# Two of nine tiles get their experts from one pass over the whole table, and the other seven are summed in quarters of the TensorE array

## What is computed

```python
def peer_block(xb, w_q, pk_keys, u_tab, v_tab):
    q = (xb @ w_q).reshape(t, PEER_HEADS, 2, PEER_DHALF)
    s = jnp.einsum('thpd,hpkd->thpk', q, pk_keys).astype(jnp.float32)
    v1, i1 = lax.top_k(s[:, :, 0], PEER_TOPK)
    v2, i2 = lax.top_k(s[:, :, 1], PEER_TOPK)
    cand = (v1[..., :, None] + v2[..., None, :]).reshape(t, PEER_HEADS, PEER_TOPK * PEER_TOPK)
    best, flat = lax.top_k(cand, PEER_TOPK)
    ...
    idx = e1 * PEER_NKEYS + e2
    g = jax.nn.softmax(best, axis=-1)
    a = jax.nn.gelu(jnp.einsum('thkd,td->thk', u_tab[idx], xb))
    return jnp.einsum('thk,thkd->td', (g * a).astype(xb.dtype), v_tab[idx])
```

## Time and profile before

| stretch of the profiled execution, us | what it is | length, us |
|---|---|---|
| 0 to 1052 | `project`, `attend`, front of group 0 | 1052 |
| 1052 to 1851 | slots of tiles 0, 1 (128 ticks), front of group 1 (3 tiles) | 799 |
| 1851 to 2910 | slots of tiles 2 to 4 (192 ticks), front of group 2 (4 tiles) | 1059 |
| 2910 to 4203 | slots of tiles 5 to 8 (256 ticks) | 1293 |
| 4203 to 4212.5 | last sums and the last store | 9.5 |

### The profile page before, as it was taken

The page is one execution under the profiler, slowest core; times in us unless marked ns, Lnnn a source line. Parts: engine busy times, 40 slices in busy tenths (PEclk is TensorE's granted clock), DMA queues, the critical chain, the costliest instruction groups (busy, mean ns, idle before and its releaser), DMA issues.

```text
span 4212.5 us, 35633 instructions
## 1 busy us (share of the span) xinstructions
PE 3563.6 (85%) x11097; PEld 1824.6 (43%) x11097; DVE 2570.1 (61%) x5586; ACT 1487.6 (35%) x3959; POOL 1673.5 (40%) x1407
## 2 busy tenths in 40 slices
PE   8999999899889988768988878986777777787777
PEld 4545665588545454323333344442333332333222
DVE  2131456612868866958777875786775776776444
ACT  2111457611334435343443335443232233223222
POOL 0000000000337667576766667666333333333332
PEclk9999889999999999879999989998989999999999
DMA  4302320044999999899999999999999999999998
GB/s 139 113 20 71 117 71 21 21 155 151 418 418 415 419 412 420 320 421 421 421 420 420 414 416 414 421 405 418 421 421 421 417 416 415 417 413 418 421 422 348
DMA packets 238014, 1394.51 MB, mean 331 GB/s; under 512 B 25840, under 2 KB 53744, under 8 KB 84976
## 3 DMA queue, kind: packets, MB, share of 16 engines
q0 software_dynamic: 165888, 1208.03, 69.5%
q1 hardware_dynamic: 71936, 184.21, 12.0%
HBM read 1364.36 MB, written 28.70 MB: 331 GB/s over the span
## 4 chain that ended last, share of the span: by engine, by line
DMA 24%; PE 17%; POOL 16%; DVE 11%; issue 9%; ACT 2%; POOLq 0%; SPq 0%; DVEq 0%; ACTq 0%
DMA ring<-in_experts_dram,idx 24%; PE ps L1443 9%; POOL side L1333 9%; POOL ring L1322 7%; DVE ring L1717 4%; PE ps L1414 3%; PE ps L1366 2%; PE ps L1391 1%; PE ps L1376 1%; ACT diag L1540 1%; DVE hot L1598 1%; DVE cand L1583 1%; DVE hot L1594 1%; DVE idx L1602 1%; ACT wgt L1531 1%
## 5 line engine op out<-in xcount | busy, mean ns | idle before, releaser
L1443 PE MATMUL ps<-ring,diag 128*128 128x512 f32 x3648 | 1816.9, 643 | 568.9 <-ACT diag L1540 555.8
L1322 POOL DMA_INDIRECT ring<-in_experts_dram,idx x1152 | 1100.7, 955 | 2043.1 <-PE ps L1443 1285.4
L1717 DVE CUSTOM_DVE_ANT_0 ring<-ring,ps 128x1024 f32<-128x1024 f32 x1152 | 1382.8, 1219 | 766.8 <-DMA ring<-in_experts_dram,idx 751.1
L1443 PEld LDWEIGHTS ps<-ring,diag 128*128 128x128 f32 x3648 | 714.5, 203 | 1582.9 <-ACT diag L1540 809.3
L1524 ACT ACTIVATE act_<-hid 128x2 f32<-128x2 f32 x576 | 117.1, 203 | 1803.4 <-DVE hid L1717 1801.8
L1333 POOL TENSOR_TENSOR side<-side,ring 128x1024 f32<-128x1024 f32 x240 | 566.9, 2362 | 55.5 <-ACT ring L1545 50.8
L1366 PE MATMUL ps<-shared 128*128 128x256 f32 (+2 forms) x1152 | 401.0, 495 | 4.5 <-PEq L536 4.5
L1540 ACT ACTIVATE diag<-const,wgt 128x128 f32<-128x128 f32 x912 | 329.8, 396 | 19.4 <-PE ps L1443 0.5
L1366 PEld LDWEIGHTS ps<-shared 128*128 128x128 f32 x1152 | 225.1, 196 | 172.6 <-issue 117.4
L316 PE MATMUL ps<-shared,hT 128*128 128x512 f32 (+1 forms) x720 | 285.4, 552 | 1.8 <-DVE mhT L430 1.3
L1531 ACT ACTIVATE wgt<-act_,gw 128x1 f32<-128x1 f32 x1152 | 276.7, 287 | 20.6 <-ACT act_ L1524 0.4
(11 more groups left out here) (181 smaller groups left out, 2854.8 us busy)
## 6 DMA issues: line engine op xcount, KB each, us to landing
shared<-in_w_gate_o_dram SPq DMA_DIRECT2D x72, 768.0 KB
shared<-in_w_q_dram SPq DMA_DIRECT2D x24, 1024.0 KB
ring<-in_experts_dram,idx POOLq DMA_INDIRECT x1152
shared<-in_w_out_dram SPq DMA_DIRECT2D x12, 1024.0 KB
shared<-in_w_in_dram SPq DMA_DIRECT2D x5, 2048.0 KB, 8.1
o_x<-o_scratch SPq DMA_DIRECT2D x9, 768.0 KB
hT_scratch<-hT SPq DMA_DIRECT2D x9, 512.0 KB, 6.6
shared<-hT_scratch SPq DMA_DIRECT2D x9, 512.0 KB
```

The costliest lines, as they stand in the source:

```text
L1322: i = nc.gpsimd.indirect_dma_start(out=ring[:, j % RING, :], out_offset=None, in_=A["experts"], in_offset=bass.IndirectOffsetOnAxis(ap=idx ...
L1443: last = nc.tensor.matmul(acc[:, h, :], diag[:, (by_pe(j) - 1) % 4, :], ring[:, j % RING, DM + h * HB:DM + (h + 1) * HB], start=(j % SLOTS ...
L1717: last = nc.vector.tensor_tensor_reduce(out=u, in0=u, in1=xp, scale=1.0, scalar=0.0, op0=ALU.mult, op1=ALU.add, accum_out=hid[:, j % SLOTS ...
```

## The change

The groups are cut differently (0-1, 2-5, 6-8). Seven tiles (`SEQ`) are still gathered, slot by slot, so that there are 448 ticks in place of 576. Tiles 3 and 5 (`DENSE`) are not gathered. Their picks and gates are ranked as before, but each pick's gate is written to a table in DRAM, `gates_scratch`, 16384 experts by 2x128 tokens: POOL issues for each of the 2x128 slots an indirect transfer of 128 elements of 4 bytes with add (`scatter`). The table is cleared early by one transfer that ACT issues in `project`. Then, from tick `DENSE_AT` = 282 on, a third list of steps (`dense`) goes over all experts in 128 blocks of 128: SP loads `u` (from a host-made transposed copy, 512 KB a block), `v` (512 KB) and the gates (128 KB); PE multiplies `u` with both tiles' tokens (8 products of 256 columns), ACT applies gelu, DVE multiplies by the gates, and PE multiplies with `v` (4 products of 512 columns) into four PSUM banks.

The gathered tiles' sums change too. The side adds are gone: all slots go to PE. `diag` is now 128x64 (a folded diagonal: two 64x64 diagonals, one above the other), and a slot is four products of 64 rows by 64 columns by 512, one in each quarter of the array, in place of two of 128 by 128 by 512. The residual comes in through PE (`residual`), `finish` is a copy, and the stores put the quarters in order. The token's row is read from SBUF (`xp`), no longer from PSUM. The ring has 9 buffers. The ranking of tiles 3, 4 and 5 is packed into 28 ticks each.

```diff
-RING = 10
+RING = 9
 BATCH = 2
 NB = SLOTS // BATCH
-GROUPS = ((0, 1), (2, 3, 4), (5, 6, 7, 8))
-PARTS = (2, 3, 4)
-SIDES = (4, 4, 3, 3, 3, 0, 0, 0, 0)
-PLAIN = SLOTS // 2
-SIDE_AT = {0: (), 3: (1, 3, 6), 4: (1, 3, 5, 7)}
+GROUPS = ((0, 1), (2, 3, 4, 5), (6, 7, 8))
+PARTS = (2, 4, 3)
+SEQ = (0, 1, 2, 4, 6, 7, 8)
+DENSE = (3, 5)
+ALL = len(SEQ) * SLOTS
...
             act.wait_ge(pad_zero, 2)
+            nc.scalar.dma_start(S["G_d"].rearrange("(p r) t -> p (r t)", p=P).rearrange("p (a b) -> p a b", b=P),
+                                S["vsw"][:, 0, :].unsqueeze(1).to_broadcast([P, NK * NK * len(DENSE) // P, P])).then_inc(S["G_zero"], 16)
...
+DENSE_AT = 282
...
+    for i in range(2 * NB, DENSE_AT):
+        to = min(total[2], mid + -(-(total[2] - mid) * (i + 1 - 2 * NB) // (G2_TICKS - 4)))
+        out.append(to - done)
+        done = to
+    ticks = len(SEQ) * NB - DENSE_AT
+    for i in range(ticks):
+        to = total[2] + -(-DENSE_STEPS.steps * (i + 1) // ticks)
...
+RANK_AT = {1: (30, 48), 3: (2 * NB + 2, 28), 4: (2 * NB + 34, 28), 5: (2 * NB + 66, 28), 7: (4 * NB + 8, 36), 8: (5 * NB + 6, 48)}
...
+SPREAD_AT = ((2 * NB + 19, 8), (2 * NB + 83, 8))
+SPREAD = {}
+for _a, (_at, _gap) in enumerate(SPREAD_AT):
+    for _k in range(SLOTS):
+        SPREAD.setdefault(_at + _k // TOPK * _gap + _k % TOPK // 3, []).append((_a, _k))
...
+                def load_gates(b):
+                    if b >= 3:
+                        sp.wait_ge(d_gated, b - 2)
+                    sp.dma_start(dg[:, b % 3], G_d[b * P:(b + 1) * P, :]).then_inc(dg_in[b % 3], 16)
+
+                def load_values(v):
+                    if v >= 3:
+                        sp.wait_ge(d_summed, v - 2)
+                    src = x1_d[DENSE[v]] if v < ND else A["experts"][(v - ND) * P:(v - ND + 1) * P, DM:2 * DM]
+                    sp.dma_start(dv[:, v % 3], src).then_inc(dv_in[v % 3], 16)
...
+            def scatter(a, j):
+                if a == 0 and j == 0:
+                    pool.wait_ge(S["G_zero"], 16)
+                if j % (SLOTS // 2) == 0:
+                    pool.wait_ge(prepared[1], prepared_by(DENSE[a], j // (SLOTS // 2) + 1))
+                if j and j % TOPK == 0:
+                    pool.wait_ge(spread[a], 16 * j)
+                i = nc.gpsimd.indirect_dma_start(out=G_d.rearrange("e (t o) -> (e t) o", o=1),
+                                                 out_offset=bass.IndirectOffsetOnAxis(ap=spot[:, a, j:j + 1], axis=0),
+                                                 in_=gd[:, a, j:j + 1], in_offset=None, compute_op=ALU.add)
+                i.then_inc(spread[a], 16)
...
-            def accumulate(m, q):
-                pe.wait_ge(diags, m * NB + q + 1)
-                if q == 0 and m:
-                    pe.wait_ge(y_ready, m)
-                for j in range(m * SLOTS + q * BATCH, m * SLOTS + (q + 1) * BATCH):
-                    if sided(j):
-                        continue
+            def dense():
+                pe.wait_ge(h_in, 16 * (NT + ND))
+                pe.wait_ge(s_kept, PH * len(GROUPS))
+                for a in range(ND):
+                    pe.wait_ge(dv_in[a], 16)
                     for h in range(2):
-                        last = nc.tensor.matmul(acc[:, h, :], diag[:, (by_pe(j) - 1) % 4, :], ring[:, j % RING, DM + h * HB:DM + (h + 1) * HB],
-                                                start=(j % SLOTS == 0), stop=(by_pe(j) == by_pe(m * SLOTS + SLOTS - 1)), skip_group_check=True)
+                        last = nc.tensor.matmul(ps[:, 4 + 2 * a + h, :], ident, dv[:, a, h * HB:(h + 1) * HB], start=True, stop=False, skip_group_check=True)
+                    last.then_inc(d_summed, 1)
+                for t in range(D.steps):
+                    if t in D.scores:
+                        b = D.scores[t]
+                        pe.wait_ge(du_in[b % 3], 16 * (b // 3 + 1))
+                        if b >= 2:
+                            pe.wait_ge(d_gelued, b - 1)
+                        for k in range(KC):
+                            last = nc.tensor.matmul(ps[:, 2 + b % 2, 0:ND * P].rearrange("p (a t) -> p a t", t=P), du[:, b % 3, k, :],
+                                                    hx[:, 0:ND, k, :], start=(k == 0), stop=(k == KC - 1))
+                        last.then_inc(d_scored, 1)
+                    if t in D.values:
+                        b = D.values[t]
+                        v = b + ND
+                        pe.wait_ge(d_gated, b + 1)
+                        pe.wait_ge(dv_in[v % 3], 16 * (v // 3 + 1))
+                        for a in range(ND):
+                            for h in range(2):
+                                last = nc.tensor.matmul(ps[:, 4 + 2 * a + h, :], dw[:, b % 3, a * P:(a + 1) * P], dv[:, v % 3, h * HB:(h + 1) * HB],
+                                                        start=False, stop=(b == NK - 1), skip_group_check=True)
+                        last.then_inc(d_summed, 1)
+                    yield
+
+            advance = walk(front, dense)
...
+            def residual(n):
+                m = SEQ[n]
+                f = FRONTS[GROUP_OF[m]]
+                if n:
+                    pe.wait_ge(y_ready, n)
+                if f.final:
...
+                    x1 = side[:, n % 2]
+                for r in range(2):
+                    rows = slice(r * HD, (r + 1) * HD)
+                    for c in range(2):
+                        nc.tensor.matmul(acc[c * HD:(c + 1) * HD, r, :], ident[rows, r * HD:(r + 1) * HD], x1[rows, c * HB:(c + 1) * HB],
+                                         start=True, stop=False, skip_group_check=True)
+
+            def accumulate(n, q):
+                pe.wait_ge(diags, n * NB + q + 1)
+                if q == 0:
+                    residual(n)
+                for j in range(n * SLOTS + q * BATCH, n * SLOTS + (q + 1) * BATCH):
+                    for r in range(2):
+                        rows = slice(r * HD, (r + 1) * HD)
+                        for c in range(2):
+                            last = nc.tensor.matmul(acc[c * HD:(c + 1) * HD, r, :], diag[rows, j % 4, :], ring[rows, j % RING, DM + c * HB:DM + (c + 1) * HB],
+                                                    start=False, stop=(j % SLOTS == SLOTS - 1), skip_group_check=True)
                     last.then_inc(pe_done, 1)
...
+                    for j in range(n * SLOTS + q * BATCH, n * SLOTS + (q + 1) * BATCH):
+                        if j >= 4:
+                            act.wait_ge(pe_done, j - 3)
+                        last = nc.scalar.activation(diag[:, j % 4, :], folded, ACT.Copy, scale=wgt[:, j % SLOTS:j % SLOTS + 1])
                     last.then_inc(diags, 1)
...
+            def dense():
+                for t in range(D.steps):
+                    if t in D.gate:
+                        b = D.gate[t]
+                        dve.wait_ge(d_gelued, b + 1)
+                        dve.wait_ge(dg_in[b % 3], 16 * (b // 3 + 1))
+                        nc.vector.tensor_tensor(dw[:, b % 3], dw[:, b % 3], dg[:, b % 3], ALU.mult).then_inc(d_gated, 1)
+                    yield
+
+            def finish(n):
+                dve.wait_ge(pe_done, (n + 1) * SLOTS)
+                if n >= 2:
+                    dve.wait_ge(y_out[n % 2], 32 * (n // 2))
+                nc.vector.tensor_copy(side[:, n % 2], acc.rearrange("p a n -> p (a n)")).then_inc(y_ready, 1)
```

More of the change, by code:

```diff
@@ L1032, in paces @@
     out = [done]
[L1033 to L1044 removed]
+    start, mid = done, total[0]
```

458 lines of the change are left out of this document (255 added, 203 removed).

## The result

Four runs of the changed kernel gave 4236.21 to 4243.42 us, median 4239.75; the kernel before has 4214.81 beside them. The ratio is 1.0083 with a 95% interval of 1.0064 to 1.0101: 0.8% slower, where 2.6% faster was forecast. The run of 14265.89 us stands outside the comparison.

A forecast was written before the change was run, and what follows sets the result against it. Transfers were to bound ticks 0 to 127, transfers and DVE with scatters on top 128 to 281, PE the rest: 1052 + 806 + 968 + 1258 + 10 + 12 = 4106, predicted as 4110 us, range 3950 to 4450.

The forecast's parts named there:

- The bytes: Whole kernel: two tiles less save 268 MB of gathers, the pass adds 151; net 117 MB, 280 us at 417 GB/s.
- B: Ticks 128 to 281, 308 slots: 883 us from transfers and DVE, plus 85 for scatters, 968 us.
- The quarters: Slot sums on PE: four quarters run at a time, 0.9 us a slot, plus 0.19 us per visit to another shape.
- C: Ticks 282 to 447, 332 slots: PE passes the transfers (1253 against 1196 us); 1258 us with the start of the pass.
- The start: Before the first dots: stays at 1052 us, with 10 us added for clearing the table.
- the clear: Clearing the gates table at the start: bytes hidden, issue on ACT taken as 10 us, upper bound 230 us.
- POOL itself has room: Scatter ticks in 128 to 281: five issues of 0.955 us make 4.8 us, six gathers in following ticks make up.
- The sign that was named for it: Ticks 147 to 273: the forecast is wrong if the DMA share falls there.
- stretch A: Ticks 0 to 127: transfers bound it at 806 us, PE under it at 718.
- the 85 us for scatters: Ticks 128 to 281: 256 scatters at a third of a microsecond each, on top of 883 us.
- the scatters hold the gathers' queue: Rival, chance 0.12: at 1.4 us a scatter, ticks 128 to 281 take 1226 us, the whole 4369, slower by 3.6%.
- The end: After the last dots: 9.5 us now, with two more copies and stores 12 us.

## Why the prediction was wrong

**What held.** *The bytes* and the pace of the transfers: without scatters B takes 888 us against 883, though the 15 us of the 883 that were put down to DVE were not seen there. *The quarters*: four at a time, 0.9 us a slot and the 0.19 of a visit; the page's 995 us for 896 slots are 1.11, in C 0.97. *C*: PE-bound at 1233 us (forecast 1258); the pass cost 942 us of PE, not 922, and the slots less than the sum had. *The start*: the first dots end at 1060 us, and at 1059 in the kernel before, so the clear, priced at 10, cost nothing.

**The step that failed: "POOL itself has room".** POOL had none: it was busy 905 of 907 us in the scatter ticks, and B took 1065 us, not 968. The sign that was named for it came, a DMA share of 0.93 in ticks 147 to 273, at 331 GB/s. The sum gave a scatter the 0.955 us of a gather's issue, five of them 4.8 us a tick and six gathers to make up for it. Three things were wrong.

1. The issue has a gap of 0.30 us behind it. My sum left it out.
2. With the add the scatter's issue takes longer. The runs show 1.16 us plain and 1.79 with the add, in the same ticks. With gathers at 0.955 + 0.30 and ticks of 5.8 us, the eight ticks leave 46.4 - 20.1 = 26.3 us for 16 scatters: POOL is the bound once one costs over 1.34 us and its gap. The add lies on the far side of that point.
3. The token's row was moved to SBUF, which the section on the change names and the prediction costs at nothing without saying so. It lengthens POOL's issues beside a dot, and is worth 87 us here. With it undone B is 981 us and the whole 4153, 1% over the forecast, most of it stretch A. B comes near the 968 of the sum, but by luck in part: the 85 us for scatters in that sum were argued from the transfers' time and not from POOL's, and POOL is full there too (671 us and 505 gaps of 0.30, in 826 us).

**The rival that came nearest** was *the scatters hold the gathers' queue*, priced at 1.4 us each and with its turning point at 0.75. The cost was 0.71 us each, so just at that point, and the direction it named came true. Its mechanism did not: but for 0.3 us nothing waited for a scatter to land, POOL was busy issuing. So the gain of the bytes went into a new bound on an engine that had been at 40%.

**Stretch A** was mis-sized by 58 us. The step that failed averaged: PE's 464 us of front over all of A gave 718, under the transfers' 806, which are 6.3 us a tick. But the front of group 1 runs from tick 26 to 123 only, and not evenly. In ticks 100 to 119 PE is full or nearly so at 8.2 and 8.8 us a tick, 44 us more than at 6.3; ticks 80 to 99, with the wait of 22.4 us for the residual, took 26 more, and ticks 26 to 79 took 4 more. In the first 26 and the last 8 ticks the transfers set 6.0 and 5.3, and these give back only 16. The sum of the larger of the two for each piece was wanted, not the larger of two sums, and the wait has no term in either.

**The end** took 19.6 us, not 12. At the last dots PE still had 12.8 us of sums and of the pass to do, and copies and stores of the two tiles stand behind them.

The misses add up: 58 in A, 97 in B, 8 at the end, less 25 in C and 2 at the start, 136 us over the sum of 4106. Of the 97 in B, 84 go away with the row's place alone.

## What to carry over

When a change gives an engine new instructions, add up that engine's issue time over the few ticks in which they are dense, with the gaps between instructions, and not its share of the whole span: POOL was at 40% and became the bound. A move of an operand between SBUF and PSUM can have a price of its own, here 87 us in either kernel; ask it of each operand that a diff moves. And work that must be done before a PE-bound stretch can begin should be judged by when it lets that stretch begin.
